# The triangular inverse of the RWKV-7 recurrence: blocks of 16x16 by substitution on VectorE, two doubling levels on TensorE

## The reference

```python
def step(S, inp):
    r_t, w_t, k_t, v_t, kk_t, a_t = inp
    sa = jnp.einsum('bhvk,bhk->bhv', S, kk_t)
    S = (S * w_t[:, :, None, :]
         - sa[..., None] * (kk_t * a_t)[:, :, None, :]
         + v_t[..., None] * k_t[:, :, None, :])
    y = jnp.einsum('bhvk,bhk->bhv', S, r_t)
    return S, y
```

## Time and profile before

| | |
|---|---|
| median of 3 runs | 2542.43 us (2539.94 to 2544.08) |
| profiled execution | 2543.07 us, its span 2541.3 us |
| PE busy | 2443.2 us (96%) |
| DVE busy | 1544.2 us (61%) |
| ACT busy | 1203.0 us (47%) |
| POOL busy | 78.4 us (3%) |
| mean share of the 16 DMA engines, weights' queue | 50.0% |

### The profile page before, as it was taken

The page is one execution under the profiler, slowest core; times in us unless marked ns, Lnnn a source line. Parts: engine busy times, 40 slices in busy tenths (PEclk is TensorE's granted clock), DMA queues, the critical chain, the costliest instruction groups (busy, mean ns, idle before and its releaser), DMA issues.

```text
span 2541.3 us, 52457 instructions
## 1 busy us (share of the span) xinstructions
PE 2443.2 (96%) x21985; PEld 2326.7 (92%) x21985; DVE 1544.2 (61%) x1843; ACT 1203.0 (47%) x1528; POOL 78.4 (3%) x69
## 2 busy tenths in 40 slices
PE   7999999996999999999999999999999999999997
PEld 7999999896989889999899999999999888999886
DVE  7577576656574445555769896554855444555444
ACT  4576353332454445664563344546544433444342
POOL 0000023400000000000000000000000000000000
PEclk9999999998999999999999999999999999999999
DMA  8355542222445554455455565555566555656554
GB/s 261 118 180 170 180 137 87 91 77 102 147 142 195 187 189 150 148 179 182 133 181 176 175 174 167 166 166 182 157 190 192 184 188 187 186 182 187 186 189 134
DMA packets 215954, 419.63 MB, mean 165 GB/s; under 512 B 16833, under 2 KB 19217, under 8 KB 215041
## 3 DMA queue, kind: packets, MB, share of 16 engines
q1 hardware_dynamic: 207232, 397.46, 50.0%
q0 software_dynamic: 2016, 10.07, 1.1%
q10 hardware_dynamic: 6512, 9.28, 1.1%
HBM read 410.47 MB, written 6.29 MB: 164 GB/s over the span
## 4 chain that ended last, share of the span: by engine, by line
PE 88%; DVE 7%; ACT 3%; issue 1%; DMA 1%; POOL 0%; SPq 0%; DVEq 0%; ACTq 0%
PE ps L482 26%; PE ps L483 26%; PE ps L484 26%; PE ps L688 4%; DVE wlo L352 2%; ACT whi L348 1%; PE ps L696 1%; PE ps L595 1%; PE ps L609 1%; DMA regions<-in_a_a 0%; DMA regions<-in_xT 0%; DVE act_lo L1897 0%; PE ps L864 0%; POOL regions L444 0%; ACT regions L1351 0%
## 5 line engine op out<-in xcount | busy, mean ns | idle before, releaser
L352 DVE TENSOR_TENSOR wlo<-wraw,whi 128x1024 fp32r<-128x1024 f32 x752 | 930.7, 1241 | 862.1 <-ACT whi L348 861.1
L482 PE MATMUL ps<-act_hi,whi 128*128 128x256 f32 (+1 forms) x4736 | 1361.2, 287 | 45.0 <-DVE act_lo L2008 12.7
L483 PE MATMUL ps<-act_lo,whi 128*128 128x256 f32 (+1 forms) x4736 | 1341.8, 283 | 0.0
L484 PE MATMUL ps<-act_hi,wlo 128*128 128x256 f32 (+1 forms) x4736 | 1340.2, 283 | 0.0
L348 ACT ACTIVATE whi<-wraw 128x1024 fp32r<-128x1024 f32 x752 | 793.9, 1059 | 1131.7 <-PE ps L484 1128.2
L482 PEld LDWEIGHTS ps<-act_hi,whi 128*128 128x128 f32 x4736 | 901.1, 190 | 52.4 <-issue 30.8
L483 PEld LDWEIGHTS ps<-act_lo,whi 128*128 128x128 f32 x4736 | 903.9, 191 | 1.3
L484 PEld LDWEIGHTS ps<-act_hi,wlo 128*128 128x128 f32 x4736 | 900.8, 190 | 0.0
L483 PE MATMUL ps<-wlo,regions_r 128*128 128x512 f32 x512 | 203.0, 396 | 0.0
L484 PE MATMUL ps<-whi,regions_r 128*128 128x512 f32 x512 | 203.0, 396 | 0.0
L482 PE MATMUL ps<-whi,regions_r 128*128 128x512 f32 x512 | 203.0, 396 | 0.0
(11 more groups left out here) (313 smaller groups left out, 1456.4 us busy)
## 6 DMA issues: line engine op xcount, KB each, us to landing
wraw<-in_a_w_in SPq DMA_DIRECT2D x128, 512.0 KB, 3.9
wraw<-in_w_up SPq DMA_DIRECT2D x128, 512.0 KB, 3.7
wraw<-in_w_down SPq DMA_DIRECT2D x128, 512.0 KB, 4.8
wraw<-in_w_in SPq DMA_DIRECT2D x112, 512.0 KB, 3.7
wraw<-in_b_w_qg SPq DMA_DIRECT2D x64, 512.0 KB, 3.7
wraw<-in_a_w_out SPq DMA_DIRECT2D x32, 512.0 KB, 4.2
wraw<-in_w_k_shared SPq DMA_DIRECT2D x32, 512.0 KB, 3.7
wraw<-in_w_v_shared SPq DMA_DIRECT2D x32, 512.0 KB, 3.6
```

The source lines that it names most:

```text
L352: nc.vector.tensor_tensor(wlo[:, q % RING], wraw[:, q % RING], whi[:, q % RING].bitcast(F32), ALU.subtract).then_inc(lo_ready, 1)
L482: mm(o, hi_s, hi_m, start=first, stop=False, skip_group_check=True)
L483: mm(o, hi_s, lo_m, start=False, stop=False, skip_group_check=True)
L484: i = mm(o, lo_s, hi_m, start=False, stop=last, skip_group_check=True)
```

## The change

Levels 0 to 3 leave TensorE. Instead:

1. The "ab" products run at half slabs 4, 6, 8 and 10. ScalarE copies them, negated, from PSUM into `TTs` (`take_ab`), and stores each chunk to DRAM (`store_ab`, 2 DMAs of 256 KB).
2. `gather_ab` reads the four diagonal 16x16 blocks of each head of a chunk back, one head and chunk per partition: 4 DMAs per chunk, each 32 partitions x 16 rows x 16 values (64 bytes). It first waits for the chunk's store.
3. VectorE inverts the four 16x16 blocks of each partition by substitution, column t = 1 to 15, a product over 4 t t elements and a sum of them, in the hooks of slabs 9 to 17 (`SUBSTITUTE_AT`). The product buffer is the first place of `AB`.
4. ScalarE stores the inverted blocks (hook 18) and scatters them into `TTs` (hooks 19 to 22): 8 DMAs per chunk, each 16 partitions x 16 heads x 16 values (64 bytes). GpSimd has cleared `TTs` and set up the identity in `inv` before, and loads `ab` back into `AB` by DMA.
5. VectorE transposes chunk 0 in hook 23 (`first_turn`), and TensorE runs levels 4 and 5 of all chunks at half slabs 48 to 63. The off-diagonal mask is applied by VectorE as it evicts y (formerly ScalarE's copy), and z is added. GpSimd has no masks any more.
6. The recurrence waits for 16 steps of `lv_t` instead of 48, and the semaphores of bonus and gate loads are merged.

```diff
-    for lv in range(6):
+    for lv in (4, 5):
         m = 1 << lv
-        parts[f"level{lv}"] = ((s // (2 * m) == t // (2 * m)) & ((t // m) % 2 == 1) & ((s // m) % 2 == 0)) * 1.0
+        parts[f"level{lv}"] = ((s // (2 * m) == t // (2 * m)) & ((s // m) % 2 == 1) & ((t // m) % 2 == 0)) * 1.0
...
+        ab_dram = nc.dram_tensor("ab_scratch", [4, CH, 2, HEADS // 2, N], F32)
+        inv_dram = nc.dram_tensor("inverse_scratch", [P, 4, 16, 16], F32)
...
-        AB, Bm, Tm, Yl = (R[:, 1, 1024 * i:1024 * (i + 1)] for i in range(4))
+        AB, Tm, Yl = [R[:, 1, 1024 * i:1024 * (i + 1)] for i in range(2)], R[:, 1, 2048:3072], R[:, 1, 3072:4096]
+        blocks = lambda t_: t_.rearrange("p (b s t) -> p b s t", b=4, s=16)
+        diag, inv, terms = blocks(Tm), blocks(Yl), R[:, 1, 0:1024]
...
-        level_steps = [("ab", 0, 0, 0), ("ab", 0, 1, 0)]
+        steps_at = [[] for _ in range(2 * 4 * SLABS + 1)]
         for c in range(4):
-            level_steps += [("pair", c, 0, 0), ("pair", c, 1, 0)]
-            for lv in range(1, 6):
-                level_steps += [("y", c, 0, lv), ("y", c, 1, lv)]
-                for f in range(2):
-                    level_steps += [("z", c, f, lv)] + [("ab", c + 1, f, 0)] * (lv == 5 and c < 3)
-        steps_at, at_ = [], 0
-        for h in range(2 * 4 * SLABS):
-            n_ = 0 if h < 7 else 2
-            steps_at.append(level_steps[at_:at_ + n_])
-            at_ += n_
-        steps_at.append(level_steps[at_:])
+            steps_at[4 + 2 * c] = [("ab", c, 0, 0), ("ab", c, 1, 0)]
+        for n_, (c, lv, kind) in enumerate((c, lv, kind) for c in range(4) for lv in (4, 5) for kind in "yz"):
+            for f in range(2):
+                steps_at[48 + n_] += [(kind, c, f, lv)]
+        SUBSTITUTE_AT = {9: range(1, 6), 10: (6, 7), 11: (8, 9), 12: (10,), 13: (11,), 14: (12,), 15: (13,), 16: (14,), 17: (15,)}
...
+        def scatter(eng, c):
+
+            for p in range(2):
+                for b in range(4):
+                    eng.dma_start(TTs[64 * p + 16 * b:64 * p + 16 * b + 16, c, :].rearrange("s (q n) -> s q n", n=N)[:, :, 16 * b:16 * b + 16],
+                                  inv_dram[32 * c + 16 * p:32 * c + 16 * p + 16, b].rearrange("q s t -> s q t")).then_inc(S["inv_loaded"], 16)
...
-            ptt = nc.gpsimd.tensor_tensor
...
+            pool.wait_ge(S["bv_stored1"], 32)
+            nc.gpsimd.memset(inv, 0.0).then_inc(S["zeroed"], 1)
+            pool.wait_ge(S["zeroed"], 1)
+            nc.gpsimd.memset(Yl.rearrange("p (b n) -> p b n", b=4)[:, :, 0:256:17], 1.0).then_inc(S["zeroed"], 1)
+            pool.wait_ge(S["rk_bc"], 4)
             for c in range(4):
-                for lv in range(6):
-                    for f in range(2):
-                        n_ = (c * 6 + lv) * 2 + f
-                        if lv == 0:
-                            pool.wait_ge(S["ab_ready"], 2 * c + f + 1)
-                        if lv == 0 and c:
-                            pool.wait_ge(S["lv_y"], (c * 5 - 1) * 2 + f + 1)
-                        if lv == 1:
-                            pool.wait_ge(S["lv_t"], n_ - 1)
-                        if lv >= 2:
-                            pool.wait_ge(S["lv_y"], (c * 5 + lv - 2) * 2 + f + 1)
-                        fs = slice(f * GW, (f + 1) * GW)
-                        ptt(Bm[:, fs].rearrange("p (h t) -> p h t", h=8), AB[:, fs].rearrange("p (h t) -> p h t", h=8),
-                            cs(f"level{lv}").unsqueeze(1).broadcast_to([P, 8, CH]), ALU.mult).then_inc(S["lv_b"], 1)
+                pool.wait_ge(S["ab_stored"], 32 * (c + 1))
+                nc.gpsimd.memset(TTs[:, c, :], 0.0).then_inc(S["zeroed"], 1)
+
+            def load_ab(c):
+                for p in range(2):
+                    pool.dma_start(AB[c % 2][side(p), :].rearrange("p (q n) -> p q n", n=N), ab_dram[c, :, p]).then_inc(S["ab_loaded"], 16)
+            load_ab(1)
+            pool.wait_ge(S["inv_ready"], 1)
+            load_ab(0)
+            for c in (2, 3):
+                pool.wait_ge(S["lv_y"], 4 if c == 2 else 9)
+                load_ab(c)
...
-                n_, m_ = (c * 6 + lv) * 2 + f, (c * 5 + lv - 1) * 2 + f
+                m_ = (c * 2 + lv - 4) * 2 + f
...
                     if c:
-                        pe.wait_ge(S["lv_ysb"], 10 * c - 1 + f)
+                        pe.wait_ge(S["ab_ready"], 2 * c - 1 + f)
...
                 if kind == "y":
-                    pe.wait_ge(S["lv_b"], n_ + 1)
+                    if c < 2:
+                        pe.wait_ge(S["ab_loaded"], 64)
+                    elif lv == 4:
+                        pe.wait_ge(S["ab_loaded"], 32 * (c + 1))
                     pe.wait_ge(S["lv_m"], m_ + 1)
-                    within_tokens(f, 4 + f, flat(Bm), flat(Tm)).then_inc(S["lv_y"], 1)
+                    if m_ < 2:
+                        pe.wait_ge(S["ab_ready"], 7 + f)
+                    else:
+                        pe.wait_ge(S["lv_ysb"], m_ - 1)
+                    within_tokens(f, 4 + f, flat(AB[c % 2]), flat(Tm)).then_inc(S["lv_y"], 1)
                 if kind == "z":
                     pe.wait_ge(S["lv_ysb"], m_ + 1)
-                    pe.wait_ge(S["lv_t"], n_ - 1)
-                    within_tokens(f, 6 + f, *((tt_, flat(Yl)) if lv < 5 else (flat(Yl), tt_))).then_inc(S["lv_z"], 1)
+                    if m_ < 2:
+                        pe.wait_ge(S["inv_loaded"], 512)
+                        pe.wait_ge(S["bvs_ready"], 4)
+                    else:
+                        pe.wait_ge(S["lv_t"], m_ - 1)
+                    within_tokens(f, 6 + f, flat(Yl), flat(TTs[:, c])).then_inc(S["lv_z"], 1)
...
-            pe.wait_ge(S["lv_t"], 48)
+            pe.wait_ge(S["lv_t"], 16)
...
+            def take_ab(c):
+
+                if c == 0:
+                    act.wait_ge(S["xs_ready"], XS["z"])
+                for f in range(2):
+                    act.wait_ge(S["ab_mm"], 2 * c + f + 1)
+                    st.do(a(TTs[:, c, f * GW:(f + 1) * GW], bank(4 + f), ACT.Copy, scale=-1.0), sig["ab_ready"])
+
+            def store_ab(c):
+                act.wait_ge(S["ab_ready"], 2 * c + 2)
+                for p in range(2):
+                    act.dma_start(ab_dram[c, :, p], TTs[side(p), c, :].rearrange("p (q n) -> p q n", n=N)).then_inc(S["ab_stored"], 16)
+
+            def gather_ab(c):
+                if c == 0:
+                    act.wait_ge(S["bv_stored0"], 32)
+                act.wait_ge(S["ab_stored"], 32 * (c + 1))
+                for b in range(4):
+                    bs = slice(16 * b, 16 * b + 16)
+                    act.dma_start(diag[32 * c:32 * c + 32, b], ab_dram[c, bs].rearrange("s p q n -> (p q) s n")[:, :, bs]).then_inc(S["ab_gathered"], 16)
+
+            def g_hook(s):
+                def hook(u):
+                    t = 8 * s + u
+                    if t == 3:
+                        bonus_store(3)
+                    if 2 <= t < 6:
+                        take_ab(t - 2)
+                    if 3 <= t < 7:
+                        gather_ab(t - 3)
+                    if 2 <= t < 6:
+                        store_ab(t - 2)
+                    if t == 18:
+                        act.wait_ge(S["inv_ready"], 1)
+                        act.dma_start(inv_dram[:], inv).then_inc(S["inv_stored"], 16)
+                    if 19 <= t < 23:
+                        if t == 19:
+                            act.wait_ge(S["inv_stored"], 16)
+                            act.wait_ge(S["zeroed"], 6)
+                        scatter(act, t - 19)
+                return hook
             for s in range(4):
...
-            for e in steps_at[-1]:
-                level(*e)
...
-            i8 = cs("ident64").unsqueeze(1).broadcast_to([P, 8, CH])
+            def substitute(t):
+
+                if t == 1:
+                    dve.wait_ge(S["ab_gathered"], 256)
+                    dve.wait_ge(S["zeroed"], 2)
+                prod = terms[:, 0:4 * t * t].rearrange("p (b s k) -> p b s k", b=4, s=t)
+                st.prev()
+                st.do(tt(prod, inv[:, :, 0:t, 0:t], diag[:, :, 0:t, t].unsqueeze(2).broadcast_to([P, 4, t, t]), ALU.mult))
+                st.prev()
+                st.do(nc.vector.tensor_reduce(inv[:, :, 0:t, t], prod, AX.X, ALU.add), sig["inv_ready"] if t == 15 else None)
+
+            def first_turn(c, f):
+                fs = slice(f * GW, (f + 1) * GW)
+                if c == 0:
+                    dve.wait_ge(S["inv_loaded"], 512)
+                else:
+                    dve.wait_ge(S["lv_y"], 4 * c - 1 + f)
+                st.do(nc.vector.transpose(Tm[:, fs], TTs[:, c, fs]), sig["lv_m"])
 
             def level(kind, c, f, lv):
-                n_, m_ = (c * 6 + lv) * 2 + f, (c * 5 + lv - 1) * 2 + f
+                m_ = (c * 2 + lv - 4) * 2 + f
                 fs = slice(f * GW, (f + 1) * GW)
-                if kind == "ab":
-                    dve.wait_ge(S["ab_mm"], 2 * c + f + 1)
-                    if c == 0:
```

(57 more changed lines are left out.)

11 lines of the change are left out of this document (1 added, 10 removed).

## The result

The changed kernel takes 2509.47 us (median; 2507.13 to 2510.38) against 2543.26 us for the kernel before on the same chip: ratio 0.9868, 95% interval 0.9856 to 0.9881. Timed a second time beside three later kernels it gave 0.9859 (0.9844 to 0.9874). The forecast was 2512 us with a range of 2492 to 2546.

What follows compares the result with a forecast made beforehand. The prediction took TensorE, busy 2443.2 of 2541.3 us, to bound the kernel. Its g-stage terms summed to 173.1 us against 203.8, 30.7 less than 2543.07, giving 2512 us with a range of 2492 to 2546.

Steps and rivals of the forecast that it cites:

- A: ScalarE's queue, hooks 3 to 6: slab splits stand behind waits for chunk stores; TensorE waits around slab 11, 6 us.
- B: Middle of slab 24: TensorE waits for the inverse's scatter and VectorE's transpose, 17 us (10 to 30).
- the clock: TensorE: two new long waits, at A and B, each bring a clock loss like the present one; 5.4 us.
- the ab products: TensorE at slabs 2 to 5: each waits until ScalarE has copied the one before out of the same banks; 1.9 us.
- Removed, on TensorE: Levels 0 to 3: 48 calls of 1.10 go, 52.8 us, with 8.7 us of GpSimd mask waits and 2.7 of clock.
- all covered: Rival: B only the 1.8 us of the transposes, scatter landing within four slabs; 2486 us, chance 0.04.
- The end: Behind the last slab of the g stage: TensorE waits 1.7 us for VectorE's split and adds, where it was 2.4.
- L: Landing time of a chunk's store in DRAM, behind the previous chunk's gather on the same queue: 6 us (3.5 to 9).
- Substitution on VectorE: Hooks 9 to 17, beside TensorE: 16.0 us of VectorE work, costed at nothing on TensorE; inverse ready at 62.1.
- The level chain: Slabs with level steps: a VectorE transpose stands ahead of y's release; 0.55 us each, seven times, 3.9 us.
- Dear packets: Slower rival, ScalarE's DMA queue: a 64-byte packet costs nearly what a 2 KB one does; 2572 us at 94 ns, chance 0.16.
- The cheap case: Rival: 12 ns a packet, L 4 us or less, A 0, B 10, one clock loss; 2497 us, chance 0.20.

Runs made afterwards that it cites:

- The removal alone: Changed kernel with the gathers, the substitution, and the store and scatter of the inverse left out: 2484.23 us, ratio 0.9774 to the kernel before.
- The chunk waits: Changed kernel with one semaphore per chunk, so the first transposes wait for chunk 0's eight scatter DMAs instead of all 32: 2505.6 us, ratio 0.9855.
- the half runs: Changed kernel with 8 heads instead of 16 in every scatter DMA, 128 runs of 64 bytes instead of 256, 32 DMAs as before: 2504.89 us, ratio 0.9849.
- the spread scatter: Changed kernel with a wait per chunk and the scatter of chunks 1 to 3 moved to hooks 23, 25 and 27: 2494.12 us, ratio 0.9811.
- GpSimd's half: Changed kernel with the scatter of chunks 2 and 3 issued by GpSimd, chunks 0 and 1 by ScalarE: 2500.73 us, ratio 0.983.
- the best version: Changed kernel with the spread scatter, gathers one hook later, and VectorE's z step ahead of its split in the last eight slabs: 2486.61 us, ratio 0.9777.

## Why the prediction was right, point by point

The total was off by 2.5 us, less than the 0.2% that a measurement tells. Part of that is luck, and one of the reasons was wrong. The g stage ran from 338.7 to 508.03, 169.3 us against a sum of 173.1, and against the 205.1 measured before. So the stage itself was put 3.8 us too long: A by 3.2, B by 2.2 and the clock by 1.2, against 0.7 too little for the ab products, 1.0 for waits behind the substitution that were put at nothing, and 1 us that no term has. A wait elsewhere, which the change doesn't touch, hid part of it. The stage began 1.7 us later than before; in these profiles TensorE's wait for the a1 load varies from 1.9 to 4.2 us without a change to that part, and was 3.9 here.

*Removed, on TensorE.* Right. The count of records and 2.08 us a pair are as before. The removal alone gave 57 us, and its g stage took 146.6 us, where the forecast's sum with all covered was 146.5 (203.8 - 57.3, 2486).

*The end.* Right: 1.74 us of wait where 1.7 was worked out (its own terms, 2.4 + 1.4 - 2.2, give 1.6).

*Ab products.* 2.6 us for 1.9.

*Round trips (A).* Present, at the place named (slabs 11 and 12), but 2.8 us instead of 6. The term that was mis-sized is L. The gathers of the four chunks in the changed kernel:

```profile
359.67 1.76 ACTq L1224 DMA_DIRECT2D regions<-ab_scratch  x2
...
366.87 2.05 ACTq L1224 DMA_DIRECT2D regions<-ab_scratch  x4
...
375.01 1.94 ACTq L1224 DMA_DIRECT2D regions<-ab_scratch  x4
...
381.52 1.93 ACTq L1224 DMA_DIRECT2D regions<-ab_scratch  x4
```

The three trips between them took 7.2, 8.1 and 6.5 us where I had 8.3 (L of 6 and six issues of 0.39): 3.2 us less in all, which is the error of A. The stores landed after 4.1 us (median), not 6. I had put half of L on the 64-byte packets of the gathers ahead; in the run that leaves the gathers out the same stores landed after 4.8, so the packets ahead cost nothing that shows. A landing of 4.1 alone would give A = 3 x 4.1 - 11.9 = 0.4; the rest is issue time: a pair of stores took 1.3 to 3.6 us on ScalarE's queue where I had 0.8, and a gather 0.5 where I had 0.39. The 3.6 came twice in this kernel and was 1.2 in five other runs with the same gathers, where A was 2 us; why is not shown.

*Substitution on VectorE.* The sum was 16.0 us and it took 18.7 for the 30 instructions themselves. The sums over k cost 7.5 us, about as worked out (8.0 with the gaps); the products cost 11.2, because one operand is read at a stride of 64 bytes: beyond the 0.16 us of the smallest, 1.76 us for 900 elements is 1.8 ns each, not 1.04. It still stayed within the lag allowed until the end: TensorE's waits for `wlo` between hook 9 and slab 24 sum to 1.0 us. The inverse was ready 63.0 us after slab 3 against 62.1 foreseen: VectorE ended hook 9 at 37.3 instead of 38.6, A having been too long, and the eight hooks behind it took 25.7 us instead of 23.5.

*Scatter (B).* 14.8 us of waits for 17, within its ends of 10 and 30, and the landing at 87 us after slab 3 for 88. But the mechanism was given wrongly. I let the packets set it (20 us to drain; 8192 at 12 ns on 16 engines are 6 us) and named the issue time as the lower end, 16.7 us. Of the 24.8 us from the last sum (418.57) to the first level product (443.37), 2.8 are the store's landing and 17.9 the four blocks of issues, 17.5 of them issuing; behind these stand only the last split, on ScalarE and on VectorE, 0.9 us of landing and a transpose. The chunk waits, the half runs, the spread scatter and GpSimd's half show this, each from its own side. 0.39 us an issue was too low (0.5), but the 1.06 us of each split that I had added between the blocks is not there: the next issue starts 0.02 us after the split has started (426.91, 426.93). The two errors nearly cancel, and the drain of 20 us came close by luck.

*The level chain.* Right: 0.56 us a slab for 0.55, and the step that the forecast named (the transpose behind the split) is the one whose move takes it away.

*Clock.* Two losses for 5.4 us were foreseen. Around the scatter the granted clock fell to its lower level, 1.2 of 2.4 GHz: TensorE's matmuls stood 0.21 us apart again, the first pair behind the wait took 3.68 us instead of 2.08. Stretches from 380 to 400, 400 to 420, 420 to 443 and 443 to 450 us (length, PE, PEld, DVE, ACT, POOL busy; granted clock, DMA share, GB/s):

```profile
380.00:400.00 20.00, 17.20 (x142) 16.66 (x141) 12.92 (x25) 10.57 (x10) 2.08 (x3) 1.00 0.85 223
400.00:420.00 20.00, 18.99 (x159) 18.58 (x158) 19.50 (x19) 6.13 (x6) 1.02 (x2) 1.00 0.62 203
420.00:443.00 23.00, 8.59 (x60) 8.12 (x59) 6.57 (x6) 5.23 (x6) 0.00 (x0) 0.69 0.85 187
443.00:450.00 7.00, 6.63 (x90) 6.41 (x92) 2.24 (x4) 0.28 (x1) 0.00 (x0) 0.56 0.35 106
```

The waits of 2.01 and 0.79 us at slabs 11 and 12 left the clock at 1.00. So there was one place of loss, 4.2 us, instead of two.

*The rivals.* Dear packets fell: 12 ns against the 65 from which it would decide. The cheap case had the right price for a packet. (The straight line through 384 B and 2 KB gives 9.6 ns for 64 B, not the 12 of the prediction; that 12 was measured is chance. And 1694 packets in 5 us are 339 per us, not 320, so 8192 beside the weights would be 24 us, not 25.6.) But it had A at nothing, where 2.8 us were measured, and its B of 10 us is shorter than the forecast's own terms allow (67.5 + 16.7 + 0.7 - 71.6 = 13.3, worked out with A at 6); 14.8 were measured. Of the signs of being wrong that the forecast named, the price of a packet thus came out at its lower edge of 12 ns or under it, on the cheap side. "All is covered" was excluded by issue time in the forecast, and rightly: it took another order of the scatter to come near it.

## What to carry to other kernels

When work moves to small DMAs, count the DMAs and their place in the issuing engine's program before the bytes: here 32 issues of 0.5 us on the engine that also prepares the weights cost more than 8192 packets of 64 bytes. Spread such issues over places where their engine has time, in the order in which their data is needed, and give each portion its own semaphore; the semaphore alone moved nothing (2505.6), with the order it gave 11 us (2494.1). And where a step is inserted ahead of a signal on an in-order engine, look at what stands in front of both: one swap gave 4 to 6 us, and the best version (2486.6 us, ratio 0.9777) is as fast as the kernel with the new work left out (2484.2, 0.9774). That doesn't make the new work free: the kernel that leaves it out has no swap.

## What the runs showed of the hardware

A packet of 64 bytes in the scatter costs 10 to 12 ns of a DMA engine, one of 384 bytes 23 and one of 2 KB 94: half the time of the next size for a sixth of its bytes. An issue of a DMA with 128 or with 256 short runs holds ScalarE nearly equally long, 0.45 and 0.47 us, against 0.33 for a plain one of 512 KB (418.61 above); single issues took 1.1 to 2.2 us, and no run shows why. A split on ScalarE does not hold back the issue behind it (426.91, 426.93). Waits of 2.01 and 0.79 us left TensorE's granted clock at 1.00; behind those of 3.67 and 11.10 it stood at its lower level. VectorE's product with one operand at a stride of 64 bytes takes 1.76 us for 900 elements and 1.09 with it contiguous.
